# Sixteen gate slabs as 512-column matmuls over the high and low part of x, one bank per column half

## What is computed

```python
def _mixer_block(xn, w_in, ..., w_branch, w_out):
    proj = xn @ w_in
    (cb, cc, cx, uv, sb_q, sb_k, sb_v, fx_q, fx_k, fx_v, f_raw, gate_raw) = jnp.split(proj, idx, axis=-1)
    y_a = _short_conv_mixer(cb, cc, cx, w_conv)
    y_b = _spatial_gating_mixer(uv, w_s, b_s, ln_g, ln_b)      # gelu, layer norm, spatial product
    y_c = _merge_heads(_stick_breaking_attention(sb_q, sb_k, sb_v))
    y_d = _merge_heads(_forgetting_attention(fq, fk, fx_v, lax.cumsum(log_f, axis=2)))
    ys = jnp.stack([y_a, y_b, y_c, y_d], axis=2)
    branches = jnp.einsum('bsnc,ncd->bsnd', ys, w_branch)
    gates = jax.nn.sigmoid(gate_raw.reshape(bsz, s, N_BRANCH, D_MODEL))
    merged = jnp.sum(gates * branches, axis=2)
    return merged @ w_out
```

## Time and profile before

| | us |
|---|---|
| median of 3 runs | 753.62 |
| lowest and highest | 753.60, 753.69 |
| the profiled execution | 753.49 |
| its span, first to last instruction | 751.7 |
| busy in it: TensorE, VectorE, ScalarE | 738.8, 516.9, 374.6 |
| mean granted TensorE clock | 0.999 of 2.4 GHz |

### The profile page before, as it was taken

One profiled execution on the slowest core, in us unless ns is written; L12 is line 12 of the kernel. 1 busy time (PEld: TensorE's weight loads), 2 busy tenths in 40 slices (PEclk: granted clock), 3 DMA queues, 4 the chain that ended last, 5 costly groups with the idle time before them and its releaser, 6 DMA issues.

```text
span 751.7 us, 12083 instructions
## 1 busy us (share of the span) xinstructions
PE 738.8 (98%) x4850; PEld 665.4 (89%) x4850; DVE 516.9 (69%) x579; ACT 374.6 (50%) x441; POOL 47.9 (6%) x63
## 2 busy tenths in 40 slices
PE   8999999999999999999999999999999999999997
PEld 8999887788888888889989999999988888888886
DVE  5679846689888888876557636675576766666673
ACT  6635466365554545555564554444445434444341
POOL 2455100100000000030000000000010000000000
PEclk9999999999999999999999999999999999999999
DMA  8846334246555545336343444446443645555431
GB/s 324 333 138 195 115 112 161 69 163 225 187 205 174 207 178 189 147 112 224 117 164 129 157 165 169 168 168 225 168 169 112 224 168 204 187 177 213 168 112 57
DMA packets 18811, 129.30 MB, mean 172 GB/s; under 512 B 2256, under 2 KB 2512, under 8 KB 3536
## 3 DMA queue, kind: packets, MB, share of 16 engines
q1 hardware_dynamic: 18768, 128.68, 47.7%
HBM read 126.57 MB, written 1.05 MB: 170 GB/s over the span
## 4 chain that ended last, share of the span: by engine, by line
PE 91%; DVE 5%; ACT 2%; POOL 1%; issue 1%; DMA 1%; SPq 0%; DVEq 0%; ACTq 0%
PE ps L1437 21%; PE ps L1412 18%; PE ps L1413 18%; PE ps L1414 18%; PE ps L1443 11%; PE ps L1401 1%; DVE xx L980 1%; DVE low L932 1%; PE ps L1535 1%; DVE h L963 1%; DMA cst<-in_cst 1%; PE ps L1565 1%; PE ps L1558 0%; ACT xx L593 0%; PE ps L1704 0%
## 5 line engine op out<-in xcount | busy, mean ns | idle before, releaser
L932 DVE TENSOR_TENSOR low<-raw,hiw 128x2048 fp32r<-128x2048 f32 x116 | 268.3, 2314 | 117.7 <-ACT hiw L563 116.7
L563 ACT ACTIVATE hiw<-raw 128x2048 fp32r<-128x2048 f32 x116 | 221.9, 1914 | 175.4 <-PE ps L1443 113.4
L1437 PE MATMUL ps<-xx,hiw 128*128 128x512 f32 x704 | 169.3, 391 | 1.4 <-DVE xx L980 1.2
L1437 PEld LDWEIGHTS ps<-xx,hiw 128*128 128x128 f32 x704 | 129.9, 188 | 29.8 <-DVE xx L980 3.5
L1412 PE MATMUL ps<-xx,hiw 128*128 128x256 f32 x512 | 146.7, 286 | 0.6 <-DVE xx L980 0.6
L1413 PE MATMUL ps<-xx,hiw 128*128 128x256 f32 x512 | 144.8, 283 | 0.0
L1414 PE MATMUL ps<-xx,low 128*128 128x256 f32 x512 | 144.8, 283 | 0.0
L1412 PEld LDWEIGHTS ps<-xx,hiw 128*128 128x128 f32 x512 | 97.9, 191 | 2.4 <-issue 1.8
L1413 PEld LDWEIGHTS ps<-xx,hiw 128*128 128x128 f32 x512 | 97.9, 191 | 0.1
L1414 PEld LDWEIGHTS ps<-xx,low 128*128 128x128 f32 x512 | 97.9, 191 | 0.0
L1443 PEld LDWEIGHTS ps<-xx,low 128*128 128x128 f32 x704 | 90.3, 191 | 3.4
(11 more groups left out here) (198 smaller groups left out, 810.4 us busy)
## 6 DMA issues: line engine op xcount, KB each, us to landing
raw<-in_slabs SPq DMA_DIRECT2D x117, 1024.0 KB, 4.8
vec<-in_vec SPq DMA_DIRECT2D x1, 1258.5 KB, 9.8
cst<-in_cst SPq DMA_DIRECT2D x1, 1220.0 KB, 14.3
h<-in_x SPq DMA_DIRECT2D x2, 512.0 KB, 3.8
arena<-arena SPq DMA_DIRECT2D x16, 64.0 KB, 2.8
out<-h SPq DMA_DIRECT2D x2, 512.0 KB, 2.6
vec<-in_vec SPq DMA_DIRECT2D x1, 229.0 KB, 5.9
cst<-in_cst SPq DMA_DIRECT2D x1, 66.0 KB, 4.4
```

Of the source, the lines that this page charges most:

```text
L563: act.activation(hiw[:, n % SPLIT, :], raw[:, n % RAW, :], ACT.Copy).then_inc(hi_made, 1)
L932: dve.tensor_tensor(low[:, n % SPLIT, :], raw[:, n % RAW, :], hiw[:, n % SPLIT, :].bitcast(F32), ALU.subtract).then_inc(lo_made, 1)
L1437: pe.matmul(banks[:, c, :], hi[:, kt, cc_], xx[:, kt].rearrange("p a b -> p (a b)"), start=kt == 0, stop=False)
```

## The change

The sixteen gate slabs go through a new form on TensorE, `gate_slab`: for each column half c a bank of its own, eight matmuls of 512 columns over `xx` and eight of 256 columns with the low part of w. VectorE gets `gate_sum`, which reduces one bank's 512 elements to 256 and writes them to `sg` (e slabs) or `sgl` (l slabs), 32 of them; it comes first in the iteration of an e slab, and ahead of the subtraction for the slab three later in mix2. ScalarE no longer copies e slabs; the sigmoid of an l slab works in place on SBUF, after both its sums. VectorE waits for the gates on a new semaphore, `late_gates`. The banks are let anew: the halves of the e slabs go through 1, 4, 0 in turn, the four halves of l2_m and l3_m have banks 4, 5, 6, 7 in every round, and the four branch products the same banks 4, 5, 6, 7. The number and order of the slabs, the loads, the FFNs, norms and attentions stay.

```diff
--- before.py
+++ after.py
@@ -274,8 +274,6 @@
         for n, b in (("sq", 0), ("sk", 1), ("sv", 0), ("fq", 6), ("fk", 7), ("fv", 1), ("cc", 0), ("cx", 1), ("cb", 0),
                      ("u", 1), ("v", 0)):
             tenant(n, b, 2 if n in ("fq", "fk") else 1)
-        for i, n in enumerate(EARLY):
-            tenant(n, (i + 1) % 2)
         for hh in range(4):
             tenant(f"ss{hh}", 2 + hh % 2)
             tenant(f"sr{hh}", 5)
@@ -289,12 +287,16 @@
             tenant(f"ft{hh}", 5)
             if hh % 2 == 0:
                 tenant(f"fo{hh // 2}", 7)
+        for i, n in enumerate(EARLY):
+            for c in range(2):
+                tenant(f"{n}_{c}", (1, 4, 0)[(2 * i + c) % 3])
         tenant("gm", 6)
         for m in range(4):
-            tenant(f"l2_{m}", 2 if m == 1 else 4)
-            tenant(f"l3_{m}", 3 if m == 1 else 5)
+            for j in range(2):
+                for c in range(2):
+                    tenant(f"l{2 + j}_{m}_{c}", 4 + 2 * j + c)
             for n in range(N_BRANCH):
-                tenant(f"br{m}_{n}", (6, 7, 4, 5)[n])
+                tenant(f"br{m}_{n}", 4 + n)
         for q in range(4):
             tenant(f"w2_{q}", q, 0)
         for q in range(4):
@@ -348,6 +350,8 @@
                 return proj_used[stage], int(name[1:]) + 1
             if stage == "mix2" and name[0] == "m":
                 return full(f"br{name[1:]}_3")
+            if name in EARLY or stage == "mix2":
+                return full(f"{name}_1")
             return full(name)
 
 
@@ -844,17 +848,9 @@
                 me.step(act, act.activation(lse, lsa, ACT.Exp, scale=-1.0))
                 act.activation(lsa, lse, ACT.Ln, bias=1.0).then_inc(s("f_ln"), 1)
 
-            def early_gate(i):
-                n = EARLY[i]
-                br, m = int(n[1]), int(n[3])
-                evacuate(n, sg[:, br, 2 * m:2 * m + 2, :])
-
-
             tables("natural_log_exp_and_others")
             for k in range(19):
-                if k >= 11:
-                    early_gate(k - 11)
-                elif IN2[k] in ("sq", "sk", "sv", "fv", "cc", "u", "v"):
+                if k < 11 and IN2[k] in ("sq", "sk", "sv", "fv", "cc", "u", "v"):
                     evacuate(IN2[k], {"sq": sqT, "sk": skT, "sv": sv, "fv": fv, "cc": cc, "u": uT, "v": vt}[IN2[k]])
                 if k in (3, 4):
                     fox_square(k - 3)
@@ -901,12 +897,14 @@
             nxt[0] = b2 + 22
             assert b2 + 22 == base + 3
             for m in range(4):
+                for n in range(2):
+                    act.wait_ge(*given_back(f"e{n}_{m}_1"))
                 act.activation(sg[:, :, 2 * m:2 * m + 2, :], sg[:, :, 2 * m:2 * m + 2, :],
                                ACT.Sigmoid).then_inc(s("early_gates"), 1)
-                if m >= 2:
-                    act.wait_ge(s("merged"), m - 1)
                 for j in range(2):
-                    evacuate(f"l{2 + j}_{m}", sgl[m % 2][:, j, :], ACT.Sigmoid)
+                    for c in range(2):
+                        act.wait_ge(*given_back(f"l{2 + j}_{m}_{c}"))
+                    act.activation(sgl[m % 2][:, j, :], sgl[m % 2][:, j, :], ACT.Sigmoid).then_inc(s("late_gates"), 1)
                     rnd_to(AT[("mix2", f"l{2 + j}_{m}")] + 3)
                 rnd_to(AT[("mix2", f"m{m}")] + 3)
                 act.wait_ge(s("merged"), m + 1)
@@ -1299,8 +1297,18 @@
                 dve.tensor_tensor(vt, vt, uT, ALU.mult).then_inc(s("yb_made"), 1)
 
 
+            def gate_sum(name, c, dst):
+
+                dve.wait_ge(*full(f"{name}_{c}"))
+                dve.tensor_reduce(dst, bank(f"{name}_{c}").rearrange("p (a b) -> p b a", a=2), AX_X, ALU.add)\
+                   .then_inc(*frees(f"{name}_{c}"))
+
             dve.memset(onesT, 1.0)
             for k in range(19):
+                if k >= 11:
+                    n = EARLY[k - 11]
+                    for c in range(2):
+                        gate_sum(n, c, sg[:, int(n[1]), 2 * int(n[3]) + c, :])
                 if 2 <= k <= 5:
                     stick_scores(k - 2)
                 if 3 <= k <= 6:
@@ -1345,7 +1353,10 @@
                     nxt[0] += 1
 
             for m in range(4):
-                res_to(AT[("mix2", f"l3_{m}")] + 3)
+                for j in range(2):
+                    for c in range(2):
+                        gate_sum(f"l{2 + j}_{m}", c, sgl[m % 2][:, j, c * T:(c + 1) * T])
+                    res_to(AT[("mix2", f"l{2 + j}_{m}")] + 3)
                 for n in range(N_BRANCH):
                     if n == N_BRANCH - 1:
                         res_to(AT[("mix2", f"m{m}")] + 2)
@@ -1353,7 +1364,7 @@
                         dve.wait_ge(s("early_gates"), m + 1)
                         gate = sg[:, n, 2 * m:2 * m + 2, :].rearrange("p a b -> p (a b)")
                     else:
-                        dve.wait_ge(*given_back(f"l{n}_{m}"))
+                        dve.wait_ge(s("late_gates"), 2 * m + n - 1)
                         gate = sgl[m % 2][:, n - 2, :]
                     dve.wait_ge(*full(f"br{m}_{n}"))
                     dst = macc[m % 2] if n == 0 else mtmp[n % 2]
@@ -1443,6 +1454,20 @@
                         mm = pe.matmul(banks[:, c, 0:T], lo[:, kt, cc_], xhi[:, kt, :], start=False, stop=kt == KT - 1)
                 return mm
 
+            def gate_slab(stage, name):
+
+                n = AT[(stage, name)]
+                hi, lo = slab_views(n, KT)
+                pe.wait_ge(lo_made, n + 1)
+                for c in range(2):
+                    take_bank(pe, f"{name}_{c}")
+                    o, cc_ = bank(f"{name}_{c}"), slice(c * P, (c + 1) * P)
+                    for kt in range(KT):
+                        pe.matmul(o, hi[:, kt, cc_], xx[:, kt].rearrange("p a b -> p (a b)"), start=kt == 0, stop=False)
+                    for kt in range(KT):
+                        mm = pe.matmul(o[:, 0:T], lo[:, kt, cc_], xhi[:, kt, :], start=False, stop=kt == KT - 1)
+                    mm.then_inc(*fills(f"{name}_{c}"))
+
             def feature_half(o, n, c):
 
                 hi, lo = slab_views(n, KT)
@@ -1750,7 +1775,10 @@
 
             for k, name in enumerate(IN2 + EARLY):
                 how = token_major if name in ("sv", "fv", "v") else feature_major
-                project("in2", name, how, 2 if k == 0 else None)
+                if name in EARLY:
+                    gate_slab("in2", name)
+                else:
+                    project("in2", name, how, 2 if k == 0 else None)
                 if k == 6:
                     for j in range(2):
                         fox_norm(j)
@@ -1786,7 +1814,7 @@
 
             for m in range(4):
                 for j in range(2):
-                    project("mix2", f"l{2 + j}_{m}", feature_major)
+                    gate_slab("mix2", f"l{2 + j}_{m}")
                 n_ = AT[("mix2", f"m{m}")]
                 pe.wait_ge(lo_made, n_ + 1)
                 if m == 0:
```

## The result

| | before | after |
|---|---|---|
| median | 753.62 | 758.57 |
| lowest and highest of 5 | 753.47, 754.87 | 757.36, 758.91 |
| the profiled execution | 753.49 | 758.57 |
| its span | 751.7 | 756.8 |
| busy: TensorE, VectorE, ScalarE | 738.8, 516.9, 374.6 | 738.8, 536.0, 370.7 |

The changed kernel is slower: ratio 1.0051, 95% interval 1.0035 to 1.0067. Its five times come in two groups, 757.36 and 757.45 with a mean granted clock of 0.999, and 758.57 to 758.91 with 0.997 or 0.998; the profiled execution is of the second.

The account below looks back on a forecast made before the run. TensorE's own work was taken to bound the kernel, with VectorE and ScalarE in cover. Waits of 6.4 us less a gain of 3.04 cost 3.4: 753.6 + 3.4 = 757.0, range 753.9 to 760.0 (own range 755.2 to 758.5).

Parts of the forecast that it names:

- The chain: mix2: sums, sigmoid, rounding, subtraction and merge over VectorE and ScalarE take 22.64 a round against TensorE's 22.41.
- C: Rival: TensorE's granted clock falls in the wait before o3, which then costs 2.7 more: 759.7; chance 0.11.
- D: Rival: the new form gives nothing when banks change at each half, the 3.04 are missing: 760.0; chance 0.04.
- VectorE's price: One VectorE reduction of 512 PSUM elements to 256, taken at 0.69 us; own range from 0.59 to 0.78.
- Slab 17: At the layer norm (k = 15): the second half of slab 17 waits 1.1 us for its bank.
- l2_1: mix2 after the first round: slab l2_1 waits 1.1 us for bank 4, held until the first branch product.
- Bank 6: mix2's later rounds: the third branch product waits for bank 6, 0.4, then 0.3 and 0.3 us.
- o3: Last round of mix2: slab o3 waits 3.2 us for the low part of the merged sum.
- The form's gain: TensorE's sixteen gate slabs: 5.57 instead of 5.76 us each, a gain of 0.19 a slab and 3.04 in all.
- The Trainium skill's 2.5 ns a matmul: TensorE's cost beside columns / 2.4 GHz; by it the form saves 0.04 us a slab, 0.64 in all.
- A: Rival: VectorE's sums are cheap enough to stay in cover; 752.8 at 0.41 each, 750.6 with full cover; chance 0.07.
- B: Rival: mix2's lag doesn't add up over rounds, VectorE's idle times absorb it; waits 3.4, time 754.0; chance 0.14.

Follow-up runs that it names:

- e3: Changed kernel with the four gate halves of mix2's round 1 in banks 0 to 3; median 758.82, ratio 1.0056.
- e10: Kernel of e7 with the FFN's order inside a slab, 16 wide matmuls of both halves first, then 16 narrow; median 750.18, ratio 0.9948.
- e8: Changed kernel with the sum of each first half in mix2 made twice on VectorE, 8 more reductions; median 763.13, ratio 1.0121.
- e6: Changed kernel with in2's part taken back, so only mix2's eight gate slabs have the new form; median 761.20, ratio 1.0087.
- e9: Kernel of e3 with 16 products of zeros on TensorE ahead of its wait for o3; median 757.54, ratio 1.0046.
- e2: Changed kernel, but in mix2 ScalarE rounds the slab three later before the gate slab's sigmoid; median 751.98, ratio 0.9975.
- e7: Changed kernel with the edits of e2, e3 and e4 together; median 750.69, ratio 0.9956.
- e4: Changed kernel with the e halves going through four banks, not three, from slab k = 14 on; median 757.66, ratio 1.0041.
- e1: Changed kernel with 12 products of zeros on TensorE ahead of its wait for o3; median 757.26, ratio 1.0039.

## Why the prediction was right, and where it was off

The chain was predicted, and the waits held term by term. The number held in part by luck. The median, 758.57, is 1.6 above the forecast of 757.0 and just outside the forecast's own range (755.2 to 758.5); the stated range covers it because it reached on to C and D. Of the 4.95 by which the medians differ, 3.7 are the waits less the form's gain; the rest goes with the lower granted clock of three of the five executions, a term that the sum put at nothing and left to C with 0.11. With one more execution of the lower group the median would have been 757.4.

- **VectorE's price.** 0.69 was taken for a sum, 0.68 to 0.69 is measured.
- **Slab 17.** Its second half would have started at 453.92 (0.95 after 452.97) and did at 455.02: 1.1, as predicted.
- **l2_1.** 481.74 against 482.94: 1.2, predicted 1.1. e3 adds what the prediction had not said: this wait is part of the one way in which VectorE's lag shows, and taking it away gains nothing.
- **Bank 6.** 0.4, 0.3, 0.3 (two matmuls take 0.61 from 496.93, 0.56 from 519.71 and 0.56 from 542.43, otherwise 0.24); predicted the same.
- **The chain.** Products start at 482.11, 502.63, 525.36, 548.08, that is 22.7 apart from round 1 on; predicted 22.64.
- **o3.** 3.2 measured, 3.2 predicted, though the prediction's own figures, 78.2 less 75.1, give 3.1.
- **The form's gain** was mis-sized: 0.19 a slab and 3.04 in all was taken from the FFN's slabs, 0.175 and 2.8 is measured (11.17 for two slabs, before 11.52). The step that failed here is that the new order has the same counts and so the same time; e10 shows that alternating wide and narrow costs 0.02 a slab. The waits sum to 6.5, less 2.8 gives 3.7, and o3 starts 3.7 late. The forecast of 757.0 stands 0.4 under the group with the clock kept; 0.25 of it is this term.
- **The Trainium skill's 2.5 ns a matmul** (TensorE: Matmul & The Clock Gate, back-to-back issue gap), a figure that the section gives for the isolated matmul, was set against the rows and left. The measured 0.175 us a slab goes against the 0.04 worked out from it, and for the rows.

The rivals. A (sums in cover) is out by the wait before o3 and by e8; B (the lag doesn't add up) by the products' spacing. C had 0.11 and is there besides the forecast, not in place of it: the clock fell in o3 in the profiled execution, and three of five times stand higher by 1.2 to 1.5, the median among them. What held it back was the argument that TensorE's idle time would hardly reach the one seen at the end; idle for 3.2, the engine did lose it in that execution.

C's price of 2.7 doesn't follow from its own rows. 0.229 against 0.118 is nearly double, so half pace throughout 5.5 us of work costs 5.2 more, and C would have stood at 762.2, outside the range. The granted clock of rows 13's stretch also reads 1.00 in the trace of before, so that row doesn't show the clock. In the trace of after the fall lasted 3.4 us of o3's 7.2 and cost 1.7; in e6's, o3 takes 8.47 (555.42 to 563.89), 3.0 more than o2 before.

The Trainium skill's advice (TensorE: Matmul & The Clock Gate, why this matters for your kernels) against idle gaps between bursts is borne out by e3 and e9. D is out: the form gives 0.175 a slab with its bank change in each.

## What to carry to other kernels

When an engine off the critical path gets work, ask where in its queue, and in the queues it feeds, the work stands: the 32 added sums (19 us busy) brought 6.5 us of waits while ScalarE's rounding stood behind a sigmoid that waits for them, 1.1 once it no longer did (e2), and none when the bank behind the layer norm was free too (e7). Idle time of an engine is not room if it waits, in that time, for a chain that its own new work lengthens. And a wait seen on TensorE is worth removing only if it lies ahead of the chain that sets the end (slab 17), not behind it (l2_1).

## What the runs showed of the hardware

After an idle time of TensorE of 3.2 us, followed by dense work, the granted clock fell to 1.2 GHz in the profiles of after (at 555.8), e3 (near 554.4, as the work resumed) and e6; o3 then took 1.7, 1.7 and 3.0 us longer than the 5.5 of o2 before. In the profiles of e4 and e8 the same idle time left the clock at 2.4 GHz. The mean granted clock suggests the fall in three of five executions of after and all seven of e3, but it doesn't say where in the kernel it came. The clock also fell elsewhere: in e4's profile right after 1.55 us of idle time at 80 us, where in the profile of before it is kept. That this idle time is the cause is not shown.

```profile
80.00:82.00 2.00, 0.61 (x5) 0.48 (x7) 1.93 (x7) 1.18 (x1) 0.00 (x0) 1.00 0.45 57
82.00:84.00 2.00, 2.00 (x12) 1.34 (x11) 1.97 (x5) 0.65 (x3) 0.00 (x0) 0.50 0.70 291
84.00:86.00 2.00, 2.00 (x13) 2.00 (x13) 2.00 (x2) 0.92 (x5) 0.00 (x0) 0.64 0.42 176
```

So a kernel's times can fall into groups though nothing in it changes (the kernel before, in the session of e1 to e4, has 13 of 28 times at 753.3 to 753.7 and 8 at 755.0 to 755.5), and the lowest execution is the one to compare when a change is worth less than their distance. Eight matmuls of 512 columns and eight of 256 in turn take 0.01 us longer for each half than sixteen and sixteen (two slabs 11.17 in e7, 11.13 in e10).
